# Decoder layer: the output projection with VectorE's list shifted by one tile, and a recurrence projection that starts on columns split earlier

## What is computed

```python
h = _ln_plain(x) * (1.0 + sc_m) + sh_m
z = h @ lw['w_in']
...                                                # sparse attention on a part of z
o_h, s_new = _hgrn2(q_h, 1.0 - fgate, jnp.log(fgate), i_h, hg_state, chunk)
o_h = o_h * lax.rsqrt(jnp.mean(jnp.square(o_h), -1, keepdims=True) + LN_EPS) * lw['hg_norm_w']
o_h = o_h * jax.nn.silu(g_h)
...
mix = (mg_a * y_a + mg_b * y_b) @ lw['w_out']
x1 = _ln_affine(DN_ALPHA * x + gt_m * mix, lw['ln1_g'], lw['ln1_b'])
h2 = _ln_plain(x1) * (1.0 + sc_f) + sh_f
f_out, conv_new = _conv_ffn(h2, conv_buf, lw['w_up'], lw['w_gate'], lw['conv_w'], lw['conv_b'], lw['w_down'])
x2 = _ln_affine(DN_ALPHA * x1 + gt_f * f_out, lw['ln2_g'], lw['ln2_b'])
```

## Time and profile before

| | |
|---|---|
| time, median of 3 runs | 2467.59 us (2463.82 to 2469.54) |
| the profiled execution | 2468.61 us, of which 2466.8 us are the span from its first to its last instruction |
| busy | PE 2243.8 us (91%), PEld 1980.2 (80%), DVE 972.5 (39%), ACT 671.2 (27%), POOL 711.9 (29%) |
| mean granted TensorE clock | 0.945 of full speed |
| prompt attention | to 913.5 us |
| recurrence projection | 915.1 to about 1115.6 us |
| output projection | 1549 to 1701.1 us |
| FFN | from 1701.3 us to the end |

### The profile page before, as it was taken

One profiled execution on the slowest core, in us unless ns is written; L12 is line 12 of the kernel. 1 busy time (PEld: TensorE's weight loads), 2 busy tenths in 40 slices (PEclk: granted clock), 3 DMA queues, 4 the chain that ended last, 5 costly groups with the idle time before them and its releaser, 6 DMA issues. The chain is left out here.

```text
span 2466.8 us, 35888 instructions
## 1 busy us (share of the span) xinstructions
PE 2243.8 (91%) x15002; PEld 1980.2 (80%) x15002; DVE 972.5 (39%) x1871; ACT 671.2 (27%) x1389; POOL 711.9 (29%) x426
## 2 busy tenths in 40 slices
PE   4896999997889969996789999998999999999997
PEld 2895777773667759996789999767989899898996
DVE  7104323223566650128932035564432322323327
ACT  2112222122465541224532221224212121121213
POOL 3113212100111112204521214254434252342426
PEclk8997999976899999996899999999999999999999
DMA  5545334216300013100032130213111020110202
GB/s 209 206 129 208 128 120 162 86 69 214 132 29 29 1 50 106 43 10 7 20 88 86 52 103 18 90 63 135 52 52 52 26 78 26 52 52 27 77 18 88
DMA packets 136616, 197.02 MB, mean 80 GB/s; under 512 B 15217, under 2 KB 105259, under 8 KB 131726
## 3 DMA queue, kind: packets, MB, share of 16 engines
q1 hardware_dynamic: 128043, 150.33, 18.9%
q0 software_dynamic: 8368, 44.12, 5.1%
q10 hardware_dynamic: 44, 0.27, 0.0%
HBM read 172.61 MB, written 26.36 MB: 81 GB/s over the span
## 5 line engine op out<-in xcount | busy, mean ns | idle before, releaser
L2872 PE MATMUL PS<-part_hi,w_ff_hi 128*128 128x344 f32 x1024 | 329.0, 321 | 0.0
L2872 PE MATMUL PS<-part_hi,w_ff_lo 128*128 128x344 f32 x1024 | 326.9, 319 | 0.0
L2872 PE MATMUL PS<-part_lo,w_ff_hi 128*128 128x344 f32 x1024 | 326.7, 319 | 0.0
L2872 PEld LDWEIGHTS PS<-part_hi,w_ff_hi 128*128 128x128 f32 x1024 | 192.5, 188 | 5.5 <-issue 5.1
L2872 PEld LDWEIGHTS PS<-part_lo,w_ff_hi 128*128 128x128 f32 x1024 | 192.2, 188 | 0.3
L2872 PEld LDWEIGHTS PS<-part_hi,w_ff_lo 128*128 128x128 f32 x1024 | 192.4, 188 | 0.0
L2994 POOL TENSOR_TENSOR w_ff_lo<-w_raw,w_ff_hi 128x1024 fp32r<-128x1024 f32 x42 | 100.6, 2396 | 282.4 <-ACT w_ff_hi L2947 282.4
L3047 DVE TENSOR_SCALAR conv_sb<-up_sb,conv_wT 128x1024 f32<-128x1024 f32 x22 | 44.2, 2010 | 280.1 <-ACT up_dec L2961 280.1
L1599 ACT ACTIVATE scores<-scores,mins_p 128x640 f32<-128x640 f32 (+5 forms) x192 | 113.4, 592 | 121.2 <-DVE mins_p L1636 121.2
L494 PE MATMUL PS<-h_hi,w_hg_parts 128*128 128x344 f32 x576 | 138.9, 324 | 7.5 <-DMA part_lo<-h_lo_rows 7.4
L2911 PE MATMUL PS<-w_down_hi,act_hi 128*128 128x512 f32 x352 | 139.7, 397 | 0.0
(11 more groups left out here) (505 smaller groups left out, 5017.6 us busy)
## 6 DMA issues: line engine op xcount, KB each, us to landing
w_or_ada<-w_ada SPq DMA_DIRECT2D x8, 2048.0 KB, 7.9
w_raw<-w_up SPq DMA_DIRECT2D x22, 512.0 KB, 4.7
w_raw<-w_gate SPq DMA_DIRECT2D x22, 512.0 KB, 4.8
w_raw<-w_down SPq DMA_DIRECT2D x22, 512.0 KB, 3.5
w_ada_sb<-w_ada SPq DMA_DIRECT2D x4, 2048.0 KB, 17.5
w_hg_raw<-w_in SPq DMA_DIRECT2D x16, 512.0 KB, 3.7
w_merge_raw<-w_in SPq DMA_DIRECT2D x16, 512.0 KB, 4.0
h_hi_rows<-h_hi SPq DMA_DIRECT2D x1, 4128.0 KB, 15.0
```

The costliest lines, as they stand in the source:

```text
L2872: last = pe.matmul(PS[:, e % BANKS, 0:cols], r(wt[:, s, k, :]), r(ht[:, k, t0:t0 + cols]), start=k + i == 0, stop=k == KD - 1 and i == 2)
```

## The change

**In `prompt_attention`** SP loads the first 128 columns of the output gate's weights (512 KB) into the then free buffer of the even heads, once head 2 is through. ScalarE makes the high part in step 26 and GpSimd the low part in step 27 of the 32.

**In `project_hgrn`** these 128 columns are unit 0, and the next 128 are unit 1, loaded and split at the start of the block; then f, q, the second half of g, and i. There are as many events and matmuls as before. TensorE starts with `high_passes` of events 0 to 2, 48 matmuls that need only the high part of h and the weights split earlier; the transpose of the lower bounds and the waits for `h_in` come behind them; events 3 to 5 (unit 1) begin with their 48 high passes, and `low_pass` is made as the pieces of h land. The copy of q's decode columns (`qd`) moves behind event 35.

**In `output_projection`** VectorE's list is shifted: `residual_norm(s)` now comes ahead of `second_norm(s - 1)`. ScalarE's list has the modulation of place s-2 (it was s-1) between its two deviations, the high part behind them, GpSimd's the low part of s-2. TensorE transposes place s-2 behind three quarters of its place instead of a half, for the decode place behind its matmuls. The row of gates and the small transposes of the convolution's constants stand between quarters of places 0 and 1. `first_feed` uses other banks and the order (0,0), (1,0), (0,1), (1,1).

The core of the diff:

```diff
@@ prompt_attention
+            sp.wait_ge(scored, 4 * NT * (HPG - 1))
+            sp.dma_start(w_raw[:, :, :], a["w_in"][0].rearrange("(k p) n -> p k n", p=P)[:, :, Z_GH:Z_GH + P]).then_inc(w_in, 16)
...
+                if n == NT * (HPG - 1) + 3:
+                    pool.wait_ge(w_high, 1)
+                    pool.wait_ge(w_in, 16)
+                    pool.tensor_tensor(r32(w_lo[:, :, :]), w_raw[:, :, :], w_hi[:, :, :], ALU.subtract).then_inc(w_low, 1)
...
+                if n == NT * (HPG - 1) + 2:
+                    act.wait_ge(w_in, 16)
+                    act.activation(r32(w_hi[:, :, :]), w_raw[:, :, :], ACT.Copy).then_inc(w_high, 1)
@@ project_hgrn
-        units = [z + 256 * i for z in (Z_FH, Z_QH, Z_GH, Z_IH) for i in range(2)]
+        units = [Z_GH, Z_GH + P] + [z + 256 * i for z, i in ((Z_FH, 0), (Z_FH, 1), (Z_QH, 0), (Z_QH, 1), (Z_GH, 1), (Z_IH, 0), (Z_IH, 1))]
+        width = [P, P] + [256] * 7
...
+            for e in range(3):
+                high_passes(e)
             pe.wait_ge(lb_in, 16)
             pe.transpose(PS[:, 7, 0:2 * HH], lbR[:, :], ident[0:2 * HH, 0:2 * HH]).then_inc(lb_mm, 1)
+            pe.wait_ge(h_in[0], 32)
+            low_pass(0)
+            weights.ready(pe, 0)
+            for e in range(3, 6):
+                high_passes(e)
+            for n in range(1, 3):
+                pe.wait_ge(h_in[n], 32)
+                low_pass(n)
+            for e in range(3, 6):
+                low_pass(e)
             pe.wait_ge(lb_ready, 1)
-            products(pe, PS, events, weights, mm_done, even_read, odd_read, h_in)
...
@@ output_projection, TensorE
-                half_rows(s, 0)
+                quarter_rows(s, 0)
+                quarter_rows(s, 1)
+                if s == 0:
+                    gate_row()
+                if s == 1:
+                    constants(1)
+                quarter_rows(s, 2)
+                if s == 0:
+                    constants(0)
...
                 if s >= 2:
                     transpose(s - 2)
-                half_rows(s, 1).then_inc(mm_done, 1)
...
+                quarter_rows(s, 3).then_inc(mm_done, 1)
@@ output_projection, ScalarE
                 deviation(s, sd, mv, stat_done, std_done)
-                deviation(s, sdb, mvb, stat2_done, std2_done)
-                if s >= 1:
-                    if s - 1 != DEC:
-                        modulate(s - 1)
-                    high(s - 1)
+                if s >= 2 and s - 2 != DEC:
+                    modulate(s - 2)
+                if s >= 1:
+                    deviation(s - 1, sdb, mvb, stat2_done, std2_done)
+                if s >= 2:
+                    high(s - 2)
@@ output_projection, VectorE
+            for s in range(LASTS):
+                if s == DEC + 3:
+                    modulate_decode()
+                residual_norm(s)
...
+                if s:
+                    second_norm(s - 1)
+            second_norm(LASTS - 1)
+            residual_norm(LASTS)
...
+            second_norm(LASTS)
```

More of the change, by code:

```diff
@@ L1433, in prompt_attention @@
          "even_read", "odd_read", "pv_done", "o_scaled", "o_added", "pool_own", "c_clear"))
+    w_raw, w_hi, w_lo = m["w_first"]
+    w_in, w_high, w_low = (sem("pt_w_" + x) for x in ("in", "high", "low"))
     toep_in, h_in = [sem("pt_toep_in0"), sem("pt_toep_in1")], sem("pt_h_in")
@@ L1741, in _, with high_passes, low_pass @@
         @block.tensor
         def _(pe):
+            def high_passes(e):
+                u, left, right, rows, cols = events[e]
+                for k in range(KD):
+                    (lh, ll), (rh, rl) = left(k), right(k)
+                    pe.matmul(PS[0:rows, e, 0:cols], r32(lh), r32(rh), start=k == 0, stop=False)
+                    pe.matmul(PS[0:rows, e, 0:cols], r32(ll), r32(rh), start=False, stop=False)
+            def low_pass(e):
+                u, left, right, rows, cols = events[e]
+                for k in range(KD):
+                    last = pe.matmul(PS[0:rows, e, 0:cols], r32(left(k)[0]), r32(right(k)[1]), start=False, stop=k == KD - 1)
+                last.then_inc(mm_done, 1)
@@ new lines, in _ @@
+            for e in range(3, 6):
+                low_pass(e)
+            pe.wait_ge(lb_ready, 1)
+            unit = 1
+            for e in range(6, NEV):
+                u, left, right, rows, cols = events[e]
+                if u != unit:
+                    unit = u
+                    weights.ready(pe, u - 1)
+                if e >= 8:
+                    pe.wait_ge(odd_read if e % 2 else even_read, e // 2 - 3)
+                product(pe, PS[0:rows, e % 8, 0:cols], left, right, KD).then_inc(mm_done, 1)
@@ L1778, in _ @@
             pool.wait_ge(weights.lo_done, 2)
-            for u in range(1, len(units)):
+            for u in range(1, len(units) - 1):
                 weights.low(pool, u, 16 * (u + 1))
@@ L1785, in _ @@
             own(v.memset(keep[:, :], 1.0))
-            weights.low(v, 0, 16)
+            weights.low(v, 0, 16, P)
             v.wait_ge(lb_mm, 1)
@@ L2461, in passes, with quarter_rows @@
                 return ((hi, wh), (hi, wl), (lo, wh))
-            def half_rows(s, half):
-                for k in range(KD):
+            def quarter_rows(s, quarter):
+                half = quarter // 2
+                for k in range(4 * (quarter % 2), 4 * (quarter % 2) + 4):
                     if half == 0 and k % 4 == 0:
@@ L2469, in half_rows, with gate_row, constants @@
                 return last
+            def gate_row():
+                pe.wait_ge(one_in, 16)
+                pe.wait_ge(gr_read, 1)
+                for half in range(2):
+                    last = pe.matmul(PS[:, 6 + half, :], one[:, :], gr[:, 512 * half:512 * half + 512], start=True, stop=True)
+                last.then_inc(gb_mm, 1)
+            def constants(part):
+                if part == 0:
+                    pe.wait_ge(k_in, 16 * 3)
+                    pe.transpose(PS[:, 4, 0:4 * FT], cwR[:, :], ident[0:4 * FT, 0:4 * FT])
+                for f in range(FT // 2 * part, FT // 2 * part + FT // 2):
+                    last = pe.transpose(PS[:, 5, 2 * NB * f:2 * NB * f + 2 * NB], old[:, P * f:P * f + P], ident[0:2 * NB, 0:2 * NB])
+                if part:
+                    last.then_inc(k_mm, 1)
             def decode_rows(s):
@@ L2498, in first_feed @@
                     for i, (wt, ht) in enumerate(((wgh, h2h), (wgh, h2l), (wgl, h2h))):
-                        last = pe.matmul(PS[:, 2 * kind + n, 0:T // 3], r32(wt[:, kind, k, :]), r32(ht[:, k, hc]), start=k + i == 0, stop=k == KD - 1 and i == 2)
+                        last = pe.matmul(PS[:, 2 * n + kind, 0:T // 3], r32(wt[:, kind, k, :]), r32(ht[:, k, hc]), start=k + i == 0, stop=k == KD - 1 and i == 2)
                 last.then_inc(ff["mm_done"], 1)
@@ L2596, in _ @@
             for s in range(len(seq)):
+                if s == LASTS:
+                    lower(s - 2)
                 r = rows[s]
@@ L2649, in modulate_decode, with residual_norm @@
                 v.tensor_tensor(d, d, adaT[:, 3 * KD:4 * KD, 0:NB], ALU.add).then_inc(h2_done, 1)
-            for s in range(len(seq)):
+            def residual_norm(s):
                 r, b = rows[s], s % 2
```

115 lines of the change are left out of this document (65 added, 50 removed).

## The result

The changed kernel takes 2454.74 us (median of 5 runs, 2452.65 to 2457.51), the one before 2467.59: ratio 0.995 (95%: 0.9937 to 0.9962), 12 us faster. In a later measurement of its own it was 2455.17 against 2467.84, ratio 0.9949 (0.9936 to 0.9963). The forecast of 2447.3 was 7.4 us too low. The result lies outside the 2443 to 2451 of the forecast's own case and inside the whole range of 2442.5 to 2457.5; the sign held.

The account below looks back on a forecast made before the run. TensorE was taken to run gapless from the FFN's start, so the gain is how much earlier that comes, with VectorE's wait for GpSimd pacing the output projection. 0 + 10.3 + 10 = 20.3 us saved gives 2447.3; range 2442.5 to 2457.5.

Parts of the forecast that it names:

- the forecast's own case: Whole kernel: the summed saving of 20.3 us holds, giving 2443 to 2451 us; chance 0.64.
- the change leaves the FFN's work as it is: FFN: only its start at 1701.4 us was to come earlier, so it got no term in the sum.
- 10.3 + 10 + 0: Forecast savings in us: 10.3 in the recurrence projection, 10 in the output projection, 0 in the attention.
- The held start: Rival, recurrence projection: pieces of h or unit 2 land 2 to 4 us later, or half clock lasts; 2449.5 to 2451.5; chance 0.10.
- the missed slot: Rival, output projection: x_norm issued after 7.90 waits for GpSimd's addition, 10 us lost, 2457.3 us; chance 0.17.
- Recurrence projection: Term for `project_hgrn`: TensorE starts at 915.15 and event 5 ends at 940.3 instead of 950.65, saving 10.3 us.
- Output projection: Term for `output_projection`: VectorE no longer waits for GpSimd's addition, most places take about 12.2 us; 10 us saved, bounds 6 and 13.
- Attention: 0: Term for `prompt_attention`: the early split's added ScalarE and GpSimd work is covered by idle time, so it costs 0.
- A sharing of bandwidth: Output projection, alternative to exclusive blocking: x_norm would end at 9.1 and each place take 0.6 us longer; no chance given.

Follow-up runs that it names:

- after: The changed kernel itself, in its profiled execution of 2452.65 us; measured at 2454.74 us, ratio 0.995 to the kernel before.
- projection alone: Kernel before the change plus only the edits of `prompt_attention` and `project_hgrn`; 2460.09 us, ratio 0.9969 to the kernel before.
- banks as before: Changed kernel with FFN tiles 1 and 2 exchanged back to their old banks, TensorE keeping the new order; 2448.5 us, ratio 0.9931 to the kernel before.
- norm after high part: Changed kernel with ScalarE's high part ahead of the second deviation, except for the decode rows, making x_norm about 1 us later; 2468.68 us, ratio 1.0005.
- decode order: Changed kernel with VectorE's `second_norm(3)` ahead of `residual_norm(4)` and ScalarE taking tile 3's deviation first in that step; 2455.38 us, ratio 0.9946.
- low part ahead: Kernel of all three edits, with GpSimd's low part of tile 2 moved ahead of its multiplication for the decode tile; 2442.91 us, ratio 0.9903.
- shift alone: Kernel before the change plus only the edits of `output_projection` and the FFN's new order of tiles; 2461.4 us, ratio 0.9978 to the kernel before.
- low passes later: Changed kernel with the recurrence projection's 96 high passes of events 0 to 5 first, then low passes piece by piece; 2453.75 us, ratio 0.9937.
- all three: Changed kernel with old FFN banks, tile 3's norm ahead of the decode residual, and low passes behind all high passes; 2446.46 us, ratio 0.9917.

## Why the prediction came out as it did

**The forgotten term.** The step that failed is "the change leaves the FFN's work as it is", by which the sum has no term for the FFN. The work is the same, but the order of its first four tiles is not, and with it which reader frees the bank of the ninth output. That cost 3.62 us of waiting and about 1.2 of half clock behind it, 4.8 in the fourth column. By the stages the miss is 4.8 + 2.6 + 1.6 = 9.0 us of 20.3, more than half of it here. The kernel with the old banks comes to 2448.5, 1.2 above the forecast; by its ratio to the kernel before on its own chip, to 2450.6, 3.3 above. Its profile saves 10.2 + 9.5 + 0.2, beside a forecast of 10.3 + 10 + 0. Over after, only the 5.0 us in the fourth column are the banks'. The 2.5 in the second and the 1.1 in the third come from the clock, which did not fall there in this execution, and from an earlier landing of h's pieces. The diff named the new banks and order, and the user of a bank seven outputs later follows from them by counting.

**The range held in part by luck.** It reached up to 2457.5 for the sake of two rivals. The held start came about, with 2.6 us, the missed slot did not, and more than half of the miss is a wait that neither rival has. The FFN's first row, foretold near 1680, did start at 1680.47, but the attention of that execution had ended 4.7 us earlier than before, which the change has no part in.

**Recurrence projection: the mechanism right, the size 0.4 to 2.4 off.** Event 5 was to end 28.5 us behind the attention (940.3 - 911.82), set by the landing of the third piece, with a wait of some tenths ahead of it. In four other executions of the same code (projection alone, banks as before, norm after high part, decode order) it is so: low pass 2 starts within 0.05 us of that landing, 0.1 to 0.4 us late, and event 5 ends 28.9 to 29.3 behind the attention. The 0.4 to 0.8 are the piece, which landed 23.5 to 23.9 us behind the attention (forecast 23.4), and four low passes that took 5.4 us instead of 5.1. In after and when it was measured again event 5 ends at 30.9 and 30.7: the third piece had landed 1.5 us ahead of low pass 2, and what set the end was the first piece, 9.6 and 9.4 us behind its issue instead of 8.5, with the half clock that followed the wait for it. The half clock at the start that I had put in (1.5 us) came in the projection alone and was hidden by the wait for the first piece, as forecast.

**Output projection: 8.4 to 9.5 instead of 10.** x_norm was issued at 7.65 (forecast 7.7 to 7.8) and ended at 8.46 (8.44), GpSimd's multiplication at 7.91 (7.90), a place takes 12.2 to 12.5 us (12.2), and place 5 was late as forecast (1615.79 - 1538.11 is 77.7 us behind the first product; forecast 1625.6 - 1550.49, 75.1). Of those 2.6 us, 1.1 are half clock in place 0, 0.6 two places that take 12.5 instead of 12.2, and 0.7 lie in the decode place: from its first copy to the end of x_norm 14.4 us (1601.36 to 1615.73) instead of 13.7, since GpSimd held up two of VectorE's operations there. From place 5 to the end of the last product it was 64.4 us, where I had 62.0 and 3 of half clock; the clock was at 0.50 for 3.2 us behind the 5.12 us wait and for as long behind the 2.44 us one at the end.

That x_norm comes just ahead of GpSimd's addition carries the gain of this stage: the kernel that makes it 1 us later loses 14 us. The rule of the Trainium skill that I leaned on (page "SBUF — State Buffer", section "Who interferes with whom": such an operation of VectorE and one of GpSimd's that reads SBUF exclude each other for a whole instruction) agrees with the traces: a norm of VectorE that had waited ends 0.55 behind GpSimd's end in after, in the kernel with the later norm and in that with the decode order. A sharing of bandwidth would not give a cost of 2.4 us for 1.

**Attention: 0** holds: from TensorE's first spread of the coefficients to the attention's end it is 270.2 to 270.4 us with the early split and 270.3 and 270.6 without it.

## What to carry to other kernels

When an edit renames or reorders outputs that live in rotating buffers, count forward to the next user of each buffer and ask which engine frees it now; the cost appears in a block that the edit doesn't touch. Where two engines exclude each other for whole instructions, place the instructions by their issue times, since a margin of 0.3 us here decided over 2.4; but on a stretch where one of them has no slack, moving the other's work only moves the loss. Compare stages from a common event, not by their absolute times, when an earlier stage wanders by 6 us.

## What the runs showed of the hardware

- Behind a wait of TensorE of 2.62 and 2.44 us ahead of the first piece of h the granted clock fell to 0.50 for some 3.4 us (two executions), which cost about 1.7 us (3.4 at half of 1.00); after 1.84, 1.96 and 2.30 us at the same place it stayed at 1.00. That the length of the wait decides isn't shown, and the next point speaks against it.
- At three other places the clock fell in some executions and not in others, with the same code ahead. Behind the 3.4 us in which the recurrence projection opens it fell in the projection alone and with the low part ahead, and in no other kernel with the early split. The first half of place 0 in the output projection takes 5.8 us in some executions (shift alone, banks as before, norm after high part, decode order, low part ahead) and 6.8 to 6.9 in others (after, in both measurements, low passes later, all three). And behind the same wait of 2.43 us at the end the clock fell to 0.50 in after, in both measurements, shift alone, banks as before, decode order and low passes later, and stayed at 1.00 with all three edits and with the low part ahead, 1.5 us. Such differences belong to no edit; I can't say what decides them.
- The first piece of h's low part landed 8.8 to 9.6 us behind its issue in the nine executions with the early split, and 8.5 in the two without, though half as many weights were asked for beside it. The next weights are asked for earlier, 4.6 to 4.9 us behind the block's first transfer instead of 6.5; whether that is why, no run tests.
- Where x_norm took the pair between two of GpSimd's operations, GpSimd's next one is shown with 2.72 us instead of 2.4: its wait is in its duration. VectorE's x_norm, issued 0.26 us ahead of the end of GpSimd's, is shown with its plain 0.81, and with 0.97 where it was issued 0.42 us ahead.
